# RMS norms of a one-core kernel: token sums as four columns, root and inverse on 128x4, spread with the repeated inverse as stationary operand

## The chip, the cores and the metric

The kernel runs on 1 core of one Trainium2 chip, as a single launch. The metric is the device time of that core in microseconds. The median of 3 runs before the change is 3313.32 us (3313.13 to 3313.98). TensorE (PE) multiplies; VectorE (DVE), ScalarE (ACT) and GpSimd (POOL) do the elementwise work; SyncE (SP) issues the weight transfers.

## The reference, cut to what matters

Three transformer blocks over 512 tokens of width 1024, in float32. What the change touches is the norm, which stands ahead of or behind nearly every branch:

```python
def rms_norm(x, g):
    xf = x.astype(jnp.float32)
    y = xf * lax.rsqrt(jnp.mean(xf * xf, axis=-1, keepdims=True) + EPS)
    return (y * g.astype(jnp.float32)).astype(x.dtype)

# one half of a layer of the second part
h = h + 0.5 * rms_norm_2(swiglu(rms_norm_2(h, g[4]), ffn_w13[i, 1], ffn_w2[i, 1]), g[5])
gate = jax.nn.sigmoid(rms_norm_2(h, g[6]) @ ple_w_gate[i])
h = h + rms_norm_2(gate * (p[i] @ ple_w_proj[i]), g[7])
```

Between these stand dilated, stick-breaking and memory attention, a gated convolution MLP, a gMLP mixer and an RWKV-7 mixer; the change leaves them as they are.

## The kernel before, in words

Activations lie features by tokens: eight tiles of 128 features x 512 tokens. Every weight product is three products of a high and a low part (`xh`, `xl` with `wh`, `wl`), so PE runs a long row of 128x512 matmuls (line 510, helper `linear`; lines 1219 to 1221, helper `Woven`). Weights come in 1 MB chunks into two slots of `raw`; ACT makes `wh` (line 315), DVE makes `wl` (line 331).

The order is written out by hand: each stage appends to a block of every engine, and semaphores with constants join them. Each engine works its own row of instructions strictly in order.

A norm is an object `Pass`. Its mean is over features, so over partitions and over the eight tiles. Where the producer of the tiles already added up squares (`by="before"`), seven tiles' squares stand in one 128x512 tile (`rs` or `sums_p`) and the last tile's squares in another (`tmp`). A second kind (`by="tensor"`) squares all eight tiles itself, and PE adds up each.

Eleven passes have the form that the change touches (`self.quarters`); they stand at about 559, 928, 1295, 1586, 1954, 2015, 2384, 2400, 2866, 3235 and 3295 us of the span:

- `sum_quarters` (lines 804 to 809, matmul at 807): four matmuls with 32 columns of ones as stationary operand and 128 tokens of squares as moving operand. Token block b gives partitions 32b to 32b+31 of a 128x128 result in bank 7, each sum 32 times over. All matmuls here are float32, and the trace shows two loads and two matmuls for each one issued.
- `square_root` (line 770, ACT) on 128x128, out of PSUM; `invert` (line 862, DVE), a reciprocal on 128x128.
- `spread` (lines 830 to 839, matmul at 837): four matmuls of 32 rows of ones with 32 rows of inverses give the inverse on all partitions, 128x512, in banks 2 and 3; a wait stands between the first two and the last two.
- `keep_busy` (line 980, matmul at 983): dummy 128x256 matmuls that fill PE while it waits for the inverse: three ahead of `spread`, and some more behind it.

Then DVE multiplies tile by tile with the spread inverse (lines 882, 885, 912), ACT takes the high part (778, 1028, 2407), DVE the low part (934, 1077), and PE starts on the first tile. In some passes POOL adds to the residual (919).

Other norms (`deferred`) already have the column form that the change brings: `add_up` (matmul at line 800), mean, root and inverse on 128x4 (866, 774, 868), diagonal and one product with ones (870, 841). They are not touched, but show operations of the same shape.

Two of the eleven passes stand in `Beside` (line 2387), where PE fills its wait not with dummies but with the products of the embedding projection, eight units of six matmuls. One (`to_hn`, line 2646, second pass) is `by="tensor"`: for each of eight tiles ACT squares (line 765), PE adds up (807), and from the third tile on PE runs two dummy matmuls ahead of each sum.

Of the kernel before, what the change touches and what calls it, by code (L numbers as in the profile page):

```python
# [219 lines left out]
def _build(nc, io, ctx, block):  # L220
# [388 lines left out]
    class Stage:  # L609
# [3 lines left out]
        def act(self, act):  # L613
            pass
# [95 lines left out]

    REPEAT = P // TB
    last_squares = [(None, act_steps)]

    class Pass:
# [3 lines left out]
        def __init__(self, number, source, gain, split=None, plain=None, onto=False, tokens=EVERY, by="tensor",  # L718
                     deferred=False, total=None, stat=0):
            self.source, self.gain, self.split, self.plain, self.onto, self.tokens = source, gain, split, plain, onto, tokens  # L720
            self.total = rs if total is None else total
            self.n_tok, self.by = tokens.stop - tokens.start, by
            self.blocks = slice(tokens.start // P, tokens.stop // P)
            self.quarters = by in ("before", "tensor") and not deferred and tokens == EVERY
            self.sums = ps[:, 7, 0:P] if self.quarters else ps[:, 7 - 5 * number, self.blocks]
            self.last, squares_by = last_squares[0]
            self.squares_sem, self.squared = squares_by.sem, squares_by.total
            self.scale = (ps[:, 2:4, P:3 * P] if self.quarters else
                          ps[:, 6 - 3 * number, tokens])
# [5 lines left out]
            for s, n in ((n_square, 0 if by == "before" else KD), (n_add, KD - 1 if by == "vector" else 0),  # L735
                         (n_sum, KD if by == "tensor" else 1), (n_mean, 0 if self.quarters else 1), (n_root, 1),
                         (n_scale, 1 if self.quarters else 2), (n_spread, 4 if self.quarters else 1),
                         (n_value, 0 if deferred else KD), (n_onto, KD if onto else 0), (n_high, KD if split else 0),
                         (n_low, KD if split else 0)):
                self.at[s] = s.total  # L740
                s.total += n
# [5 lines left out]
        def view(self, x):  # L747
            return x.rearrange("p (a t) -> p a t", a=2) if self.quarters else x

# [29 lines left out]

        def act(self, act, before):  # L780
            act.wait_ge(chunks_used, self.multiplied)
            act.wait_ge(psum_read.sem, self.evicted)
            act.wait_ge(dve_steps.sem, self.summed)
            for t in range(0 if self.by == "before" else KD):
                self.square(act, t, before)
            self.square_root(act)
            if self.split:
                for t in range(KD):
                    self.high(act, t)

        def sum_tile(self, pe, t):
            self.wait(pe, n_square, t + 1)
            if self.quarters:
                self.sum_quarters(pe, self.scratch(t % 2), t == 0, t == KD - 1).then_inc(n_sum.sem, 1)
                return
            self.add_up(pe, self.scratch(t % 2), t == 0, t == KD - 1)
# [6 lines left out]

        def sum_quarters(self, pe, squares, first_one, last_one):
            for b in range(TB):
                rows = slice(REPEAT * b, REPEAT * b + REPEAT)
                last = nc.tensor.matmul(ps[rows, 7, 0:P], table("ones")[:, 0:REPEAT], squares[:, b * P:(b + 1) * P],
                                        start=first_one, stop=last_one, skip_group_check=True)
            return last

        def sum_up(self, pe, between=0):
            if self.quarters and self.by == "before":
                pe.wait_ge(dve_steps.sem, self.summed - 1)
                self.sum_quarters(pe, self.total, True, False)
                pe.wait_ge(self.squares_sem, self.squared)
                self.sum_quarters(pe, self.last, False, True).then_inc(n_sum.sem, 1)
                return
# [24 lines left out]

        def pe(self, pe, idle, between):
            if not self.quarters:
                pe.wait_ge(psum_read.sem, self.evicted)
            self.sum_up(pe, between)
            if self.quarters:
                pe.wait_ge(psum_read.sem, self.evicted)
# [10 lines left out]
        def invert(self, dve):  # L859
            if self.quarters:  # L860
# [13 lines left out]
        def value(self, dve, t):  # L874
            g = vec[:, self.gain + t:self.gain + t + 1]
            if t == 0:
                self.wait(dve, n_spread, 4 if self.quarters else 1)
            if (self.onto or self.split) and t >= 2:
# [28 lines left out]
        def gained(self, dve, t):  # L907
            if t == 0:
                self.wait(dve, n_spread, 4 if self.quarters else 1)
            if t >= 2:  # L910
# [74 lines left out]
    class Deferred(Stage):  # L985
# [45 lines left out]
        def pe(self, pe):  # L1031
            if self.post:
# [97 lines left out]
    def split_norm(gain, source=None, split=x_split, tokens=EVERY):  # L1130
        return Norms(dict(source=h if source is None else source, gain=gain, split=split, tokens=tokens), idle=(3, 4), lead=5)

# [245 lines left out]
    def _(dve):  # L1378
        nc.vector.memset(spare[:, 0:2], 1.0)
        nc.vector.memset(spare[:, 3:4], REPEAT * REPEAT * EPS)  # L1380
        nc.vector.memset(spare[:, 2:3], GN_EPS).then_inc(halved, 1)
# [1005 lines left out]
    class Beside(Deferred):  # L2387
# [8 lines left out]

        def act(self, act):
            act.wait_ge(chunks_used, self.multiplied)
            act.wait_ge(psum_read.sem, self.evicted)
            act.wait_ge(dve_steps.sem, self.two.summed)  # L2400
            self.post.square_root(act)
            self.lots.high(act, 0)
# [9 lines left out]
        def pe(self, pe):  # L2412
# [209 lines left out]
    def rwkv():  # L2622
# [22 lines left out]

        to_hn = Norms(post(ybuf, 1, 1), dict(source=h, gain=gain(1, 2), plain=hn), idle=(3, 7, 6), between=2)
        hn_pass = to_hn.passes[1]
# [1078 lines left out]
    def _(pe):  # L3726
# [3 lines left out]
        pe.wait_ge(psum_read.sem, last.evicted)  # L3730
        keep_busy(pe, 3)
        last.spread(pe)
# [90 lines left out]
```

## Time and profile before

| what | value |
|---|---|
| median of 3 runs | 3313.32 us |
| span of the profiled execution (first to last instruction) | 3311.6 us |
| granted TensorE clock, mean | 0.995 |
| PE busy | 3236.2 us (98%) |
| DVE busy | 1780.1 us (54%) |
| ACT busy | 1214.9 us (37%) |
| POOL busy | 97.2 us (3%) |
| matmuls of line 510, share of the chain that ended last | 70% |

The profile gives the profiled execution no total of its own beside the span; the median of the runs lies 1.7 us above the span, which is what start and end outside the first and last instruction take. PE's share counts the dummy matmuls too, and the busy time of pipelined matmuls overlaps, so 98% does not say that PE never waits. The granted clock is 1.0 for 2.4 GHz and 0.50 for 1.2 GHz.

### The profile page before, as it was taken

Reading aid. Unit: us, or ns where it says so; the run is one execution under the profiler, and the core shown is the slowest. Engines: PE = TensorE matmul, PEld = TensorE weight load, DVE = VectorE, ACT = ScalarE, POOL = GpSimd, SP = SyncE. Lnnn points to the kernel's source line nnn. Section 1 sums busy time; section 2 is a strip of 40 time slices with the busy share of each in tenths; the row PEclk is TensorE's granted clock in tenths of the full one; section 3 lists DMA queues with packets and bytes.
Section 4 is the critical chain, followed back from the end, with each engine's and each line's share of the span. In section 5 each row is a group of like instructions: output and inputs, shape, how many; then the busy total and the mean of one; then the engine's idle time right before and its main releaser. Section 6 shows DMA issues by size and latency. Waiting matters only on the chain.

```text
span 3311.6 us, 46921 instructions
## 1 busy us (share of the span) xinstructions
PE 3236.2 (98%) x20532; PEld 2650.2 (80%) x20532; DVE 1780.1 (54%) x2113; ACT 1214.9 (37%) x1532; POOL 97.2 (3%) x100
## 2 busy tenths in 40 slices
PE   8999999999999999999999999999999999999998
PEld 6878786888878888988788887888777787788886
DVE  5446665776254434464644357443476665754437
ACT  3347643322242223342422234222235564332224
POOL 2000000000000001000100011000000000100001
PEclk9999999999999999999999999999999999999999
DMA  5211131222322223222222222222212100122231
GB/s 189 84 52 64 64 140 42 99 102 87 104 90 102 85 96 112 102 77 102 83 102 93 88 99 89 95 97 88 92 70 73 50 4 16 70 103 101 87 104 64
DMA packets 45980, 286.49 MB, mean 87 GB/s; under 512 B 5952, under 2 KB 6224, under 8 KB 19920
## 3 DMA queue, kind: packets, MB, share of 16 engines
q1 hardware_dynamic: 44240, 280.34, 24.2%
q0 software_dynamic: 1536, 3.15, 0.4%
q8 instruction: 162, 2.65, 0.3%
q14 instruction: 42, 0.34, 0.0%
HBM read 278.22 MB, written 2.10 MB: 85 GB/s over the span
## 4 chain that ended last, share of the span: by engine, by line
PE 80%; DVE 5%; ACT 1%; issue 1%; DVEq 0%; ACTq 0%
PE ps L510 70%; PE ps L3245 3%; PE ps L3283 1%; PE ps L1219 1%; DVE wl L331 1%; PE ps L983 1%; DVE xl L2719 1%; PE ps L1220 0%; PE ps L1221 0%; ACT wh L315 0%; PE ps L2549 0%; DVE xl L1077 0%; PE ps L837 0%; DVE tmp L2727 0%; PE ps L3290 0%
## 5 line engine op out<-in xcount | busy, mean ns | idle before, releaser
L510 PE MATMUL ps<-xh,wh 128*128 128x512 f32 (+1 forms) x2464 | 966.6, 393 | 23.3 <-DVE xl L1077 10.6
L510 PE MATMUL ps<-xl,wh 128*128 128x512 f32 (+1 forms) x2464 | 947.1, 391 | 0.3
L510 PE MATMUL ps<-xh,wl 128*128 128x512 f32 (+1 forms) x2464 | 921.3, 391 | 0.0
L331 DVE TENSOR_TENSOR wl<-raw,wh 128x2048 fp32r<-128x2048 f32 (+1 forms) x284 | 591.4, 2082 | 452.8 <-ACT wh L315 452.6
L315 ACT CAST wh<-raw 128x2048 fp32r<-128x2048 f32 (+2 forms) x281 | 487.7, 1735 | 299.0 <-PE ps L510 292.8
L510 PEld LDWEIGHTS ps<-xh,wh 128*128 128x128 f32 (+1 forms) x2464 | 463.1, 188 | 132.6 <-issue 28.0
L510 PEld LDWEIGHTS ps<-xl,wh 128*128 128x128 f32 (+1 forms) x2464 | 462.6, 188 | 101.5 <-DVE xl L1077 2.9
L510 PEld LDWEIGHTS ps<-xh,wl 128*128 128x128 f32 (+1 forms) x2464 | 462.6, 188 | 99.1 <-issue 1.0
L510 PE MATMUL ps<-hid_h,wh 128*128 128x512 f32 x880 | 342.8, 390 | 0.0
L510 PE MATMUL ps<-hid_l,wh 128*128 128x512 f32 x880 | 342.4, 389 | 0.0
L510 PE MATMUL ps<-hid_h,wl 128*128 128x512 f32 x880 | 342.4, 389 | 0.0
L2202 ACT ACTIVATE tmp<-tmp 128x512 f32<-128x512 f32 x88 | 55.7, 633 | 539.5 <-DVE tmp L2210 539.4
L2210 DVE TENSOR_TENSOR tmp<-ps,rs 128x512 f32<-128x512 f32 x88 | 60.8, 691 | 292.4 <-PE ps L510 287.0
L510 PEld LDWEIGHTS ps<-hid_h,wh 128*128 128x128 f32 x880 | 165.2, 188 | 35.3 <-DVE wl L331 1.4
L510 PEld LDWEIGHTS ps<-hid_l,wh 128*128 128x128 f32 x880 | 165.2, 188 | 34.4
L510 PEld LDWEIGHTS ps<-hid_h,wl 128*128 128x128 f32 x880 | 165.2, 188 | 34.3
L919 POOL TENSOR_TENSOR h<-tmp,h 128x512 f32<-128x512 f32 x42 | 66.5, 1613 | 2743.1 <-DVE tmp L912 2743.1
L1270 DVE COPY ybuf<-ps 128x512 f32<-128x512 f32 x40 | 27.7, 692 | 178.0 <-PE ps L510 156.4
L2195 DVE TENSOR_TENSOR hid_l<-tmp,hid_h 128x512 fp32r<-128x512 f32 x110 | 76.2, 693 | 75.5 <-ACT hid_h L2191 75.5
L1314 ACT ACTIVATE tmp<-ybuf 128x512 f32<-128x512 f32 x35 | 22.1, 632 | 246.4 <-DVE ybuf L1270 192.1
L2191 ACT CAST hid_h<-tmp 128x512 fp32r<-128x512 f32 x110 | 68.3, 621 | 86.6 <-DVE tmp L2215 67.1
L510 PE MATMUL ps<-wh,xh 128*128 128x256 f32 x352 | 94.7, 284 | 0.1
(437 smaller groups left out, 3996.2 us busy)
## 6 DMA issues: line engine op xcount, KB each, us to landing
raw<-in_up SPq DMA_DIRECT2D x88, 1024.0 KB, 4.7
raw<-in_down SPq DMA_DIRECT2D x64, 704.0 KB, 4.0
raw<-in_up_c SPq DMA_DIRECT2D x22, 1024.0 KB, 4.7
raw<-in_down_c SPq DMA_DIRECT2D x16, 704.0 KB, 4.1
raw<-in_gates SPq DMA_DIRECT2D x8, 1024.0 KB, 4.7
raw<-in_gv SPq DMA_DIRECT2D x8, 1024.0 KB, 4.8
raw<-in_gu SPq DMA_DIRECT2D x8, 1024.0 KB, 4.8
raw<-in_gout SPq DMA_DIRECT2D x8, 1024.0 KB, 4.7
```

The lines of the kernel that those rows point to most:

```text
L315: nc.scalar.copy(wh[:, slot, 0:w], raw[:, slot, 0:w]).then_inc(hi_ready, 1)
L331: nc.vector.tensor_tensor(wl[:, slot, 0:w], raw[:, slot, 0:w], wh[:, slot, 0:w].bitcast(F32), ALU.subtract).then_inc(lo_ready, 1)
L510: last = nc.tensor.matmul(out, stationary, moving, start=(fresh and q == 0), stop=(t == kt - 1 and half == per - 1 and q == 2), skip_group ...
L919: nc.gpsimd.tensor_tensor(dst, self.scratch(2 + t % 2), dst, ALU.add).then_inc(n_onto.sem, 1)
L983: nc.tensor.matmul(ps[:, bank_, 0:2 * P], table("ident"), const[:, 0:2 * P], start=True, stop=True)
L1219: nc.tensor.matmul(ps[:, b, :], wh[0:r, slot, wc], hi[0:r], start=(t == 0), stop=False, skip_group_check=True)
L2191: nc.scalar.copy(hid_h[:, k, tokens], tmp[:, 2 + u, tokens]).then_inc(act_steps.sem, 1)
L2195: nc.vector.tensor_tensor(hid_l[:, k, tokens], tmp[:, 2 + u, tokens], hid_h[:, k, tokens].bitcast(F32), ALU.subtract).then_inc(dve_steps.s ...
L2202: nc.scalar.activation(tmp[:, u, :], tmp[:, u, :], ACT.Silu).then_inc(act_steps.sem, 1)
L2210: nc.vector.tensor_tensor(tmp[:, u, :], products[0], rs[:, :], ALU.mult).then_inc(dve_steps.sem, 1)
L2719: nc.vector.tensor_tensor(xl[:, t, :], tmp[:, t % 4, :], xh[:, t, :].bitcast(F32), ALU.subtract).then_inc(x_used.sem, 1)
L3245: last = nc.tensor.matmul(out(e, c), left(lhs, e, c), right(rhs, e, c), start=(n == 0), stop=(n == len(pairs) - 1), skip_group_check=True)
```

## The change

Each of the eleven passes keeps its place. The sums become four columns: the squares of 128 tokens are the stationary operand and one column of ones the moving one, so the result is 128 tokens x 4. Root and reciprocal work on 128x4. The spread takes one column of the inverse, repeated 128 times by a stride of zero, as stationary operand and the identity as moving one, four times, with no wait between them. The dummies ahead of the spread go from three to one. In ACT's row the root is put ahead of the waits for the last chunk and the last eviction. In `Beside` one unit of products instead of two stands ahead of the spread, and the other moves behind it. Line numbers shift a little: the sum is line 808 there, the root 769, the spread 835, the dummies 981, the embedding products 1217 to 1219.

```diff
...
-            self.quarters = by in ("before", "tensor") and not deferred and tokens == EVERY
-            self.sums = ps[:, 7, 0:P] if self.quarters else ps[:, 7 - 5 * number, self.blocks]
+            self.by_columns = by in ("before", "tensor") and not deferred and tokens == EVERY
+            self.sums = ps[:, 7, 0:TB] if self.by_columns else ps[:, 7 - 5 * number, self.blocks]
...
         def square_root(self, act):
-            if self.quarters:
+            if self.by_columns:
                 self.wait(act, n_sum, KD if self.by == "tensor" else 1)
-                nc.scalar.activation(self.total[:, 0:P], self.sums, ACT.Sqrt, scale=REPEAT * REPEAT / D,
+                nc.scalar.activation(self.root, self.sums, ACT.Sqrt, scale=1.0 / D,
                                      bias=spare[:, 3:4]).then_inc(n_root.sem, 1)
...
         def act(self, act, before):
+            if self.by == "before":
+                self.square_root(act)
             act.wait_ge(chunks_used, self.multiplied)
             act.wait_ge(psum_read.sem, self.evicted)
             act.wait_ge(dve_steps.sem, self.summed)
...
-        def sum_quarters(self, pe, squares, first_one, last_one):
+        def sum_columns(self, pe, squares, first_one, last_one):
             for b in range(TB):
-                rows = slice(REPEAT * b, REPEAT * b + REPEAT)
-                last = nc.tensor.matmul(ps[rows, 7, 0:P], table("ones")[:, 0:REPEAT], squares[:, b * P:(b + 1) * P],
-                                        start=first_one, stop=last_one, skip_group_check=True)
+                last = nc.tensor.matmul(self.sums[:, b:b + 1], squares[:, b * P:(b + 1) * P], table("ones")[:, 0:1],
+                                        start=(first_one and b == 0), stop=last_one, skip_group_check=True)
             return last
...
         def spread(self, pe):
-            if self.quarters:
+            if self.by_columns:
                 self.wait(pe, n_scale, 1)
-                for n, b in enumerate((0, 2, 1, 3)):
-                    if n == 2:
-                        self.wait(pe, n_spread, 2)
-                    rows = slice(REPEAT * b, REPEAT * b + REPEAT)
-                    nc.tensor.matmul(ps[:, 2 + b // 2, P + b % 2 * P:2 * P + b % 2 * P], table("ones")[rows, :],
-                                     self.total[rows, P:2 * P], start=True, stop=True, skip_group_check=True).then_inc(n_spread.sem, 1)
+                for b in range(TB):
+                    nc.tensor.matmul(ps[:, 2 + b // 2, P + b % 2 * P:2 * P + b % 2 * P], self.inverse[:, b:b + 1].broadcast_to([P, P]),
+                                     table("ident"), start=True, stop=True, skip_group_check=True).then_inc(n_spread.sem, 1)
...
         def invert(self, dve):
-            if self.quarters:
+            if self.by_columns:
                 self.wait(dve, n_root, 1)
-                nc.vector.reciprocal(self.total[:, P:2 * P], self.total[:, 0:P]).then_inc(n_scale.sem, 1)
+                nc.vector.reciprocal(self.inverse, self.root).then_inc(n_scale.sem, 1)
...
         def split_act(self, act):
             if self.here:
                 self.here(act)
+            if self.post:
+                self.post.square_root(act)
             act.wait_ge(chunks_used, self.multiplied)
             act.wait_ge(psum_read.sem, self.evicted)
             act.wait_ge(dve_steps.sem, self.two.summed)
-            if self.post:
-                self.post.square_root(act)
...
                 pe.wait_ge(psum_read.sem, self.evicted)
-                keep_busy(pe, 3)
+                keep_busy(pe, 1)
                 self.post.spread(pe)
...
             self.lots.products(pe, 1, 0, 2)
-            self.lots.products(pe, 2, 0, 2)
             self.post.spread(pe)
-            for unit in range(3, KD):
+            for unit in range(2, KD):
                 self.lots.products(pe, unit, 0, 2)
...
```

PE's row in the two passes of `to_hn` before the change (`rs` and `tmp` are squares, `const` the ones or the dummies' operands):

```order
L807 MATMUL ps<-rs_56,const_58 32x128 x4
L807 MATMUL ps<-tmp_57,const_58 32x128 x4
L983 MATMUL ps<-const_58 128x256 x3
L837 MATMUL ps<-rs_56,const_58 128x128 x4
L983 MATMUL ps<-const_58 128x256 x6
L807 MATMUL ps<-tmp_57,const_58 32x128 x8
L983 MATMUL ps<-const_58 128x256 x2
L807 MATMUL ps<-tmp_57,const_58 32x128 x4
```

And the same place in the changed kernel:

```order
L808 MATMUL ps<-const_58,rs_56 128x1 x4
L808 MATMUL ps<-const_58,tmp_57 128x1 x4
L981 MATMUL ps<-const_58 128x256
L835 MATMUL ps<-const_58,stats_59 128x128 x4
L981 MATMUL ps<-const_58 128x256 x6
L808 MATMUL ps<-const_58,tmp_57 128x1 x8
L981 MATMUL ps<-const_58 128x256 x2
L808 MATMUL ps<-const_58,tmp_57 128x1 x4
```

Nothing moved here but the count of dummies ahead of the spread, three to one; the two dummies ahead of each later sum stay.

PE's row around the spread in the first `Beside` before the change (`pt_h`, `pt_l` are the embedding's halves). The two sums stand three rows further up, ahead of unit 1:

```order
L1219 MATMUL ps<-pt_h_7512,wh_51 128x512
L1220 MATMUL ps<-pt_l_7513,wh_51 128x512
L1221 MATMUL ps<-pt_h_7512,wl_52 128x512
L1219 MATMUL ps<-pt_h_7512,wh_51 128x512
L1220 MATMUL ps<-pt_l_7513,wh_51 128x512
L1221 MATMUL ps<-pt_h_7512,wl_52 128x512
L1219 MATMUL ps<-pt_h_7512,wh_51 128x512
L1220 MATMUL ps<-pt_l_7513,wh_51 128x512
L1221 MATMUL ps<-pt_h_7512,wl_52 128x512
L837 MATMUL ps<-rs_56,const_58 128x128 x4
```

And in the changed kernel, from the sums to the spread:

```order
L808 MATMUL ps<-const_58,rs_56 128x1 x4
L808 MATMUL ps<-const_58,tmp_57 128x1 x4
L1217 MATMUL ps<-pt_h_7509,wh_51 128x512
L1218 MATMUL ps<-pt_l_7510,wh_51 128x512
L1219 MATMUL ps<-pt_h_7509,wl_52 128x512
L1217 MATMUL ps<-pt_h_7509,wh_51 128x512
L1218 MATMUL ps<-pt_l_7510,wh_51 128x512
L1219 MATMUL ps<-pt_h_7509,wl_52 128x512
L835 MATMUL ps<-const_58,stats_59 128x128 x4
```

The spread stands six matmuls behind the sums instead of twelve; those six stand behind it now, and PE's work in the stage stays the same but for the forms of sum and spread.

## Rows read from the trace of the kernel before

**Rows 1.** The page: chain that ended last, by engine

```profile
PE 80%; DVE 5%; ACT 1%; issue 1%; DVEq 0%; ACTq 0%
```

**Rows 2.** Line 862, the reciprocals: duration ns min/median/max, first and last start

```profile
L862 DVE RECIPROCAL rs<-rs x9: 952/953/954, 560.5 to 3236.2; 128x128 f32<-128x128 f32 x9
L862 DVE RECIPROCAL sums_p<-sums_p x2: 954/954/954, 2015.9 to 3296.0; 128x128 f32<-128x128 f32 x2
```

**Rows 3.** Timeline, pass at 559: start us, us, engine, line [idle before <-releaser]

```profile
558.83 0.42 PE L807 MATMUL ps<-rs,const 128*32 128x128 f32 x8
...
559.42 0.43 PE L807 MATMUL ps<-tmp,const 128*32 128x128 f32 x8 [0.16 <-ACT tmp L1326]
...
559.99 0.37 ACT L770 ACTIVATE rs<-ps,spare 128x128 f32<-128x128 f32 x1 [0.63 <-PE ps L807]
560.50 0.95 DVE L862 RECIPROCAL rs<-rs 128x128 f32<-128x128 f32 x1 [1.85 <-ACT rs L770]
...
561.50 1.07 PE L837 MATMUL ps<-rs,const 32*128 32x128 f32 x8 [0.17 <-DVE rs L862]
...
562.65 1.41 DVE L885 SCALAR_TENSOR_TENSOR tmp<-h,vec,ps 128x512 f32<-128x512 f32 x2 [1.20 <-PE ps L837]
```

**Rows 4.** Lines 774 and 868, root and reciprocal of the untouched norms

```profile
L774 ACT ACTIVATE stats<-stats x10: 203/205/206, 31.6 to 3266.4; 128x4 f32<-128x4 f32 x9, 128x2 f32<-128x2 f32 x1
L868 DVE RECIPROCAL stats<-stats x10: 166/178/179, 31.8 to 3266.6; 128x4 f32<-128x4 f32 x9, 128x2 f32<-128x2 f32 x1
```

**Rows 5.** Timeline, column sums of an untouched norm among weight products, 3265 to 3266

```profile
3264.95 0.39 PE L510 MATMUL ps<-xh,wl 128*128 128x512 f32 x1
3265.17 0.94 PE L800 MATMUL ps<-const,rs 128*128 128x1 f32 x8
...
3265.98 2.57 PE L510 MATMUL ps<-xh,wl 128*128 128x512 f32 x10
3266.16 0.16 DVE L866 TENSOR_SCALAR stats<-ps 128x4 f32<-128x4 f32 x1 [1.23 <-PE ps L800]
```

**Rows 6.** Timeline of PE, four 128x128 by 128x128 products at 2591

```profile
2591.47 1.09 PE L3283 MATMUL ps<-const,x_area 128*128 128x128 f32 x8 [0.24 <-DVE x_area L3018]
```

**Rows 7.** Timeline, pass at 1295, whose last tile is copied out of PSUM

```profile
1294.49 0.42 PE L807 MATMUL ps<-tmp,const 128*32 128x128 f32 x8 [0.39 <-ACT tmp L1326]
...
1295.24 0.37 ACT L770 ACTIVATE rs<-ps,spare 128x128 f32<-128x128 f32 x1 [0.81 <-DVE ybuf L1270]
```

**Rows 8.** Timeline, second pass of to_hn

```profile
2392.19 0.43 PE L807 MATMUL ps<-tmp,const 128*32 128x128 f32 x8
2392.54 0.73 PEld L983 LDWEIGHTS ps<-const 128*128 128x128 f32 x4 [0.20 <-issue]
...
2399.27 0.42 PE L807 MATMUL ps<-tmp,const 128*32 128x128 f32 x8
...
2399.76 0.37 ACT L770 ACTIVATE rs<-ps,spare 128x128 f32<-128x128 f32 x1 [1.47 <-PE ps L807]
```

**Rows 9.** Timeline, the first Beside

```profile
1953.83 0.39 PE L1221 MATMUL ps<-pt_h,wl 128*128 128x512 f32 x1
...
1954.73 0.50 PE L1219 MATMUL ps<-pt_h,wh 128*128 128x512 f32 x1
...
1957.39 0.39 PE L1221 MATMUL ps<-pt_h,wl 128*128 128x512 f32 x1
...
1958.72 0.50 PE L1219 MATMUL ps<-pt_h,wh 128*128 128x512 f32 x1
...
1974.80 0.75 DVE L1077 SCALAR_TENSOR_TENSOR xl<-h,vec,xh 128x512 fp32r<-128x512 f32 x1 [0.31 <-ACT xh L2407]
...
1976.12 0.62 PE L510 MATMUL ps<-xl,wh 128*128 128x512 f32 x2
```

**Rows 10.** Stretches: us, busy us of PE, PEld, DVE, ACT, POOL, PEclk, DMA share

```profile
2405.50:2408.80 3.30, 1.18 (x5) 1.04 (x6) 3.23 (x7) 0.75 (x2) 0.00 (x0) 1.00 0.01 2
2409.00:2415.50 6.50, 5.57 (x14) 4.07 (x13) 6.36 (x12) 1.27 (x3) 0.00 (x0) 0.50 0.01 3
```

More of the change, by code:

```diff
@@ L723, in __init__ @@
             self.blocks = slice(tokens.start // P, tokens.stop // P)
-            self.quarters = by in ("before", "tensor") and not deferred and tokens == EVERY
-            self.sums = ps[:, 7, 0:P] if self.quarters else ps[:, 7 - 5 * number, self.blocks]
+            self.by_columns = by in ("before", "tensor") and not deferred and tokens == EVERY
+            self.sums = ps[:, 7, 0:TB] if self.by_columns else ps[:, 7 - 5 * number, self.blocks]
             self.last, squares_by = last_squares[0]
             self.squares_sem, self.squared = squares_by.sem, squares_by.total
-            self.scale = (ps[:, 2:4, P:3 * P] if self.quarters else
+            self.scale = (ps[:, 2:4, P:3 * P] if self.by_columns else
                           ps[:, 6 - 3 * number, tokens])
@@ L735, in __init__ @@
             for s, n in ((n_square, 0 if by == "before" else KD), (n_add, KD - 1 if by == "vector" else 0),
-                         (n_sum, KD if by == "tensor" else 1), (n_mean, 0 if self.quarters else 1), (n_root, 1),
-                         (n_scale, 1 if self.quarters else 2), (n_spread, 4 if self.quarters else 1),
+                         (n_sum, KD if by == "tensor" else 1), (n_mean, 0 if self.by_columns else 1), (n_root, 1),
+                         (n_scale, 1 if self.by_columns else 2), (n_spread, 4 if self.by_columns else 1),
                          (n_value, 0 if deferred else KD), (n_onto, KD if onto else 0), (n_high, KD if split else 0),
@@ L747, in view @@
         def view(self, x):
-            return x.rearrange("p (a t) -> p a t", a=2) if self.quarters else x
+            return x.rearrange("p (a t) -> p a t", a=2) if self.by_columns else x
         def wait_result(self, engine, t):
@@ L783, in act @@
             act.wait_ge(dve_steps.sem, self.summed)
-            for t in range(0 if self.by == "before" else KD):
-                self.square(act, t, before)
-            self.square_root(act)
+            if self.by != "before":
+                for t in range(KD):
+                    self.square(act, t, before)
+                self.square_root(act)
             if self.split:
@@ L792, in sum_tile @@
             self.wait(pe, n_square, t + 1)
[L793 to L794 removed]
+            if self.by_columns:
+                self.sum_columns(pe, self.scratch(t % 2), t == 0, t == KD - 1).then_inc(n_sum.sem, 1)
                 return
@@ L802, in add_up @@
             last.then_inc(n_sum.sem, 1)
-        def sum_quarters(self, pe, squares, first_one, last_one):
+        def sum_columns(self, pe, squares, first_one, last_one):
             for b in range(TB):
-                rows = slice(REPEAT * b, REPEAT * b + REPEAT)
-                last = nc.tensor.matmul(ps[rows, 7, 0:P], table("ones")[:, 0:REPEAT], squares[:, b * P:(b + 1) * P],
-                                        start=first_one, stop=last_one, skip_group_check=True)
+                last = nc.tensor.matmul(self.sums[:, b:b + 1], squares[:, b * P:(b + 1) * P], table("ones")[:, 0:1],
+                                        start=(first_one and b == 0), stop=last_one, skip_group_check=True)
             return last
         def sum_up(self, pe, between=0):
-            if self.quarters and self.by == "before":
+            if self.by_columns and self.by == "before":
                 pe.wait_ge(dve_steps.sem, self.summed - 1)
-                self.sum_quarters(pe, self.total, True, False)
+                self.sum_columns(pe, self.total, True, False)
                 pe.wait_ge(self.squares_sem, self.squared)
-                self.sum_quarters(pe, self.last, False, True).then_inc(n_sum.sem, 1)
+                self.sum_columns(pe, self.last, False, True).then_inc(n_sum.sem, 1)
                 return
@@ L843, in pe @@
         def pe(self, pe, idle, between):
-            if not self.quarters:
+            if not self.by_columns:
                 pe.wait_ge(psum_read.sem, self.evicted)
             self.sum_up(pe, between)
-            if self.quarters:
+            if self.by_columns:
                 pe.wait_ge(psum_read.sem, self.evicted)
@@ L876, in value @@
             if t == 0:
-                self.wait(dve, n_spread, 4 if self.quarters else 1)
+                self.wait(dve, n_spread, 4 if self.by_columns else 1)
             if (self.onto or self.split) and t >= 2:
@@ L908, in gained @@
             if t == 0:
-                self.wait(dve, n_spread, 4 if self.quarters else 1)
+                self.wait(dve, n_spread, 4 if self.by_columns else 1)
             if t >= 2:
@@ L1130, in split_norm @@
     def split_norm(gain, source=None, split=x_split, tokens=EVERY):
-        return Norms(dict(source=h if source is None else source, gain=gain, split=split, tokens=tokens), idle=(3, 4), lead=5)
+        return Norms(dict(source=h if source is None else source, gain=gain, split=split, tokens=tokens), idle=(1, 4), lead=5)
     s_high, s_low = roles("split_highs", "split_lows")
@@ L1379, in _ @@
         nc.vector.memset(spare[:, 0:2], 1.0)
-        nc.vector.memset(spare[:, 3:4], REPEAT * REPEAT * EPS)
+        nc.vector.memset(spare[:, 3:4], EPS)
         nc.vector.memset(spare[:, 2:3], GN_EPS).then_inc(halved, 1)
@@ L2397, in act @@
         def act(self, act):
+            self.post.square_root(act)
             act.wait_ge(chunks_used, self.multiplied)
@@ L2644, in _ @@
                 nc.gpsimd.memset(x[64:P, 0:2, :].bitcast(F32), 0.0).then_inc(lora_rows_clear, 1)
-        to_hn = Norms(post(ybuf, 1, 1), dict(source=h, gain=gain(1, 2), plain=hn), idle=(3, 7, 6), between=2)
+        to_hn = Norms(post(ybuf, 1, 1), dict(source=h, gain=gain(1, 2), plain=hn), idle=(1, 7, 6), between=2)
         hn_pass = to_hn.passes[1]
@@ L3730, in _ @@
         pe.wait_ge(psum_read.sem, last.evicted)
-        keep_busy(pe, 3)
+        keep_busy(pe, 1)
         last.spread(pe)
```

4 lines of the change are left out of this document (1 added, 3 removed).

## Prediction

> **What bounds the kernel now.** I read the page's chain first: 80% of what ended last is PE and 5% DVE [rows 1], so the time is PE's row of weight products plus the places where PE waits. Then the single lines of the norm, for how many passes there are: nine reciprocals on `rs` and two on `sums_p`, 0.95 us each, eleven passes [rows 2]. Then the timeline of one pass, to see whether the norm is hidden. It is not: from the last square on, every step names the one before it as its releaser. The sum starts at 559.42, the root at 559.99, the reciprocal at 560.50, the spread at 561.50, the first tile's scaling at 562.65 [rows 3]. That is 3.23 us in a line, and PE does only dummies meanwhile. What follows (scaling, high part, low part, first product) hangs on 562.65, and PE is the bound again behind it, so what such a pass gains or loses moves all that follows. This holds for nine passes. In the two of `Beside` PE has real products to do all along [rows 9], and there only PE's own work counts.
>
> **Root and reciprocal.** The root took 0.37 us on 128x128 [rows 3]; on 128x4 in the untouched norms it takes 0.205 [rows 4]: -0.165. Those read SBUF and the new one reads PSUM, so the price lies between 0.205 and 0.37; I take 0.205, since the form is otherwise the same. The reciprocal goes from 0.953 to 0.178 [rows 2, 4]: -0.775. Its form is exact. Together -0.94 a pass.
>
> **The sums on the path.** The old groups are short: eight matmuls in 0.43 us, and the root starts 0.57 us behind their start [rows 3]. The new form already stands in an untouched norm [rows 5]: eight passes of 128x128 by one column hold PE from 3265.17 to 3265.98, 0.81 us, and their reader on DVE starts 0.99 us behind their start. The reader is now ACT, which started 0.14 us after the end of the old sum, where DVE in rows 5 started 0.05 after it (3265.17 + 0.94 = 3266.11): 0.09 more. And the squares are now the stationary operand, whose load can't begin before they are there: some 0.04. So 1.12 us in place of 0.57: +0.55, bounded by 0.99 (nothing more) and about 1.2 (the 1.09 us of eight 128x128 passes [rows 6] and ACT's 0.14).
>
> The Trainium skill (TensorE: Matmul & The Clock Gate, "Part 3: Packing small matmuls — row/col tiling") speaks against this part: products that use 32 columns of the array each run side by side, and one that takes all 128 columns has no such neighbour. Its section on LDWEIGHTS has the load cost go with the columns of the stationary operand, 107 ns for 128 and so 27 for 32. By that the added time on PE would be 8 x 0.08 = 0.64 us a sum, an estimate from that page; rows 3 and 5 make it 0.4 to 0.55, since the old sum does not shrink as far as the page lets it.
>
> **The first group of sums.** It holds seven tiles and was out of the way early. At 559 it starts at 558.83 and the second at 559.42 [rows 3]; with 0.81 us it ends at 559.64, so the second waits 0.22 more. In the other passes the two groups stand about 0.8 us or more apart and nothing is added (0.8 us in rows 7 too, as I read that timeline).
>
> **The spread.** Before, from its start to its reader: 561.50 to 562.65, 1.15 us, with the wait in its middle [rows 3]. The new one is four full products of 128 columns, for which rows 6 have 1.09 us, and 0.08 to the reader as before: 1.17, +0.02. No row shows a stationary operand with stride zero. From below, nothing can be gained beyond some 0.1 (the loads alone). From above, I bound a pass by the slowest regular one near here, the dummies of 256 columns: four in 0.86 us, 0.214 each [rows 8] (0.73 us for four loads, of which the last begins 0.64 behind the first). Eight of them would be 1.71 instead of 0.86, +0.85 a spread. I take the value of rows 6, the nearest form.
>
> **Dummies three to one.** One dummy is 0.43 us. Between the end of the sum and the spread now lie 0.14 + 0.205 + 0.14 + 0.178 + 0.05 = 0.71 us (the steps between engines from rows 3), so a single one ends before the spread is due and three would not. It costs nothing, and it saves a delay that three would bring.
>
> **ACT's root ahead of its waits.** In passes whose last tile is copied out of PSUM the root waited for that copy: 1294.49 to 1295.24, 0.75 us instead of 0.57 [rows 7]. There the new sum comes 0.37 later (1.12 - 0.75), not 0.55, since the wait for the copy is gone or covered. Four passes are of this kind (1295, 1586, 2384, 2866). What is behind the root in ACT's row is the 1.9 us cast of weights, which is done well ahead of the first high part; it moves by 0.2 to 0.4 us and stays hidden.
>
> **The pass that adds on PE (2387 to 2400).** Sums follow one another at (2399.27 - 2392.19)/5 = 1.416 us, of which 0.86 are dummies and 0.35 the sum, the rest a gap in PE's row [rows 8]. With 0.81 for the sum and no gap (rows 5 show none on either side) it is 1.67. The sums of rows 8 have no idle time in front of them, so PE already is the slower one and not the squares, and it is clearly so with longer sums: six periods, 6 x 0.254 = +1.52. Then the last sum: the root came 0.49 us behind its start [rows 8], now 1.12: +0.63. Less 0.94 and plus 0.02 for the spread: +1.23.
>
> **Beside.** PE's products follow at 0.23 us. The two sums held PE from 1953.83 + 0.23 to 1954.73, 0.67 us [rows 9]; now 1.62: +0.95. The spread held it from 1957.62 to 1958.72, 1.10 us; now about 0.9: -0.2. The chain through the inverse doesn't matter: the root can start at 1956.0, the inverse is there at about 1956.6, and PE reaches the spread, behind the sums and one unit (1.36 us), at about 1957.05. Behind it the chain through the weights' cast on ACT and their low part on DVE shifts the scaling by up to 1 us, and PE by +0.75; the last low part was there at 1975.55, PE took it at 1976.12 [rows 9], so 0.57 of slack covers the difference. Result: +0.75 each, +1.5 for two. Moving the unit behind the spread brings nothing, since PE does the same work.
>
> **The sum.** Passes 928, 2015, 3295: -0.94 + 0.55 + 0.02 = -0.37, three times -1.1. Pass 559: -0.37 + 0.22 = -0.15. Four copy passes: -0.94 + 0.37 + 0.02 = -0.55, together -2.2. Pass 2400: +1.23. Two Beside: +1.5. Total -0.7 us: the profiled execution's span of 3311.6 goes to 3310.9, and with the 1.7 us that the median lies above the span, 3312.6 us. The gain in root and reciprocal, 9 x 0.94 = 8.5 us, is given back by sums that are longer on the path (4.3), by the adding pass's longer periods (1.5) and by Beside (1.5), and 0.2 each by the first group and the spreads.
>
> **Rivals.**
> *The one-column sums cost the path nothing.* If loads of the squares ran as short as the old packed ones, each of nine passes would keep -0.9 and the adding pass and Beside would lose nothing: -8.3, so 3305.0. For it: the sum is only four results. Against it: rows 5, 0.94 us for the very form.
> *The clock falls in a norm.* From 2405.5 on PE had little to do (1.18 us busy of 3.30), and from 2409.0 to 2415.5 the granted clock stood at 0.50, the lower level of 1.2 GHz [rows 10]. The changed passes put 1.6 us of one-column sums and about 0.3 us of idle time where there were three dummies. If that is too little work to hold 2.4 GHz, PE-bound products behind a norm run at half pace for a time as long as in rows 10, 6.5 us, and lose half of it, 3.3 us. It decides the sign from the first such fall on (-0.7 + 3.3); I price it at four of the eight passes that PE-bound work follows: +13 - 0.7, so 3325.6. Against it: no pass of before but 2400's has the lower level behind it, and PE does not stand idle longer than it did. No row says whether one-column matmuls hold the clock. The Trainium skill (the same page, "Part 4: PE-mode transpose") says of transposes that they don't count as busy in the same way; it has nothing on one-column products. The phase also matters: the low stretch of rows 10 comes at another moment after the change, and may shrink or grow by up to 2 us with no meaning.
> *Repeated column or root from PSUM slow.* Spreads at +0.85 in nine passes and roots at 0.37 in nine: +7.7 + 1.5 - 0.7 = +8.5, so 3321.8. For it: no row shows either. Against it: the operand's address pattern is plain, and 128x128 loads differ little over the trace.
>
> **How the numbers follow.** Forecast 0.80, the sums free 0.05, the clock 0.09, the slow spread 0.06. A measurement tells 0.2% from no change, 6.6 us. The forecast's own terms leave +-0.1 us in nine sums, up to 1.5 in the roots, 1 in the adding pass and 2 for the clock's phase: 3309.0 to 3316.5. A little toward either side makes the range 3308.5 to 3317.5. Faster by over 0.2% (under 3306.7) takes the sums' rival and little else: 0.05. Slower (over 3319.9) takes the most of the other two and single mishaps: 0.11. Same: 0.84.
>
> **What the new profile would show.** Reciprocals of 0.18 us and roots of 0.2 us on 128x4. From a second sum's start to the root about 1.1 us, and from there to the first scaling about 1.7. Sums in the adding pass at 1.67 us. Beside longer by 0.7 to 0.8 us from the first sum to the first gate product. The clock at 1.00 in all passes but the one place. I am wrong if the root starts within 0.8 us of the sum's start, if a spread takes more than 1.4 us, if the adding pass keeps 1.4 us, or if 0.50 appears behind a norm.

## The result, and the profile after

| kernel | median us | runs | ratio to before, 95% interval |
|---|---|---|---|
| before | 3312.68 (3310.52 to 3313.98) | 10 | |
| changed | 3322.54 (3313.70 to 3330.98) | 10 | 1.0028 (1.0019 to 1.0036) |

The change makes the kernel 9.9 us slower, where 0.7 us faster (3312.6 us) was forecast, and it scatters the runs over 17 us where they lay within 3.5. The profiled execution took 3321.13 us (span 3319.3), with a mean granted clock of TensorE of 0.992 against 0.995. The run list gives each run's clock: the three runs at 3313.70 to 3314.11 have 0.996, the seven from 3320.95 up have 0.989 to 0.992. That points at the clock.

An ordinary pass gains, as it was meant to. This is the pass at 926 in the timeline of the changed kernel (start us, us, engine, line); [rows 3] is its like:

```profile
925.50 1.05 PE L808 MATMUL ps<-const,tmp 128*128 128x1 f32 x8 [0.72 <-ACT tmp L1324]
...
926.59 0.26 ACT L769 ACTIVATE stats<-ps,spare 128x4 f32<-128x4 f32 x1 [1.14 <-PE ps L808]
926.98 0.18 DVE L860 RECIPROCAL stats<-stats 128x4 f32<-128x4 f32 x1 [2.26 <-ACT stats L769]
927.22 1.16 PE L835 MATMUL ps<-const,stats 128*128 128x128 f32 x8
...
928.41 2.06 DVE L883 SCALAR_TENSOR_TENSOR h<-h,vec,ps 128x512 f32<-128x512 f32 x3 [1.25 <-PE ps L835]
```

From the second sum's start to the first scaling it is 2.91 us. The same pass took 3.23 us before (927.47 to 930.70), as the one in [rows 3] did. The root comes 1.09 us behind the sum (1.12 forecast), takes 0.26 (0.205 forecast, 0.37 the other bound), the reciprocal 0.18, spread to reader 1.19 us.

The loss is in the adding pass. PE and ACT in its middle in the changed kernel, which [rows 8] answer:

```profile
2394.62 1.71 PE L808 MATMUL ps<-const,tmp 128*128 128x1 f32 x8
...
2396.18 2.05 PE L981 MATMUL ps<-const 128*128 128x256 f32 x4
2396.42 0.63 ACT L764 ACTIVATE tmp<-h 128x512 f32<-128x512 f32 x1 [2.78 <-PE ps L808]
...
2398.03 1.71 PE L808 MATMUL ps<-const,tmp 128*128 128x1 f32 x8
...
2408.27 1.71 PE L808 MATMUL ps<-const,tmp 128*128 128x1 f32 x8
...
2410.31 0.18 DVE L860 RECIPROCAL stats<-stats 128x4 f32<-128x4 f32 x1 [12.71 <-ACT stats L769]
```

A tile takes 2398.03 - 2394.62 = 3.41 us, where it took 1.416, and DVE sits idle for 12.71 us ahead of the second reciprocal. From the first reciprocal of `to_hn` (2383.06, in the same timeline) to the second it is 27.25 us; before it was 2384.57 to 2400.16, 15.59 us. Those 11.7 us are more than the whole loss. Some of them come back right behind the pass, where the low stretch of [rows 10] is gone: from the first product of line 510 to the first copy out of PSUM on DVE it is 35.61 us (2418.09 to 2453.70), and it was 37.51 (2407.62 to 2445.13). The stretches of the changed kernel (columns as in [rows 10]; PEclk is the granted clock) say why the pass is long:

```profile
2390.00:2413.00 23.00, 23.00 (x84) 20.61 (x83) 7.90 (x11) 3.41 (x6) 0.00 (x0) 0.50 0.13 46
2413.50:2440.00 26.50, 23.48 (x101) 18.09 (x100) 22.89 (x42) 6.85 (x9) 0.00 (x0) 1.00 0.00 1
```

From 2390 on PE counts as busy in every microsecond of the pass, and its granted clock is 0.50, the level of 1.2 GHz, to the end of it. PE does not look idle in any busy share; only the clock column and the durations show it (a sum's eight matmuls take 1.71 us; at the full level they took 0.95 to 1.05). Nor had PE done less ahead of the fall than before the change. These are the stretches from the last spread to it, first in the changed kernel, then the like in the kernel before:

```profile
2384.30:2389.50 5.20, 4.76 (x31) 4.01 (x29) 4.91 (x8) 1.94 (x4) 0.00 (x0) 1.00 0.00 0
2386.60:2392.20 5.60, 4.69 (x36) 3.18 (x34) 5.38 (x9) 1.89 (x3) 0.00 (x0) 1.00 0.01 3
```

PE was busy for 4.76 of 5.20 us where it had been busy for 4.69 of 5.60, with the same six dummies in it; what differs is the form of the sums. Then the clock fell in the one and stayed at 1.00 in the other.

`Beside` behaves as worked out. PE in the changed kernel:

```profile
1951.70 0.95 PE L808 MATMUL ps<-const,rs 128*128 128x1 f32 x8
...
1954.89 1.05 PE L835 MATMUL ps<-const,stats 128*128 128x128 f32 x8
...
1963.99 0.39 PE L510 MATMUL ps<-xh,wh 128*128 128x512 f32 x1
```

From the sums' turn to the first gate product it is 12.29 us; before it was 11.59 (from 1954.06, 0.23 behind the last product of [rows 9] ahead of the sums, to the first product of line 510 at 1965.65): +0.70, with +0.75 forecast.

### The profile page after: what moved, and what is told of

Same layout as the page of the kernel before. It is cut to its first block, busy times and chain, and to the rows that moved or that the text cites. A ratio compares the mean times of both kernels' runs of the same rounds, so it can differ in the third digit from the quotient of the medians.

```text
span 3319.3 us, 46841 instructions
## 1 busy us (share of the span) xinstructions
PE 3249.7 (98%) x20496; PEld 2676.7 (81%) x20496; DVE 1771.4 (53%) x2113; ACT 1214.0 (37%) x1532; POOL 97.3 (3%) x100
## 4 chain that ended last, share of the span: by engine, by line
PE 81%; DVE 4%; ACT 1%; issue 1%; DVEq 0%; ACTq 0%
PE ps L510 70%; PE ps L3242 3%; PE ps L3280 1%; PE ps L808 1%; PE ps L981 1%; DVE wl L331 1%; PE ps L1217 1%; DVE xl L2716 1%; PE ps L1219 0%; PE ps L1218 0%; ACT wh L315 0%; PE ps L2546 0%; PE ps L835 0%; DVE xl L1075 0%; DVE tmp L2724 0%
```

## The experiments

In all of them the new form and the old one stand side by side, chosen by the number of the pass in order of time (0 to 10; 7 is the adding pass, 4 and 9 are the two of `Beside`). Where a pass is in the old form its three dummies ahead of the spread are too; the root keeps its new place in ACT's row in all of them, which makes 3.37 us instead of 3.40 from sum to scaling in the old pass at 1295 (adding pass only, 1294.81 to 1298.18). Theory: the one-column sums don't hold TensorE's clock, and in the adding pass, where they alternate with dummies, it stays down. Rival: PE simply has more to do.

| kernel | median us | range | ratio to before, 95% interval |
|---|---|---|---|
| adding pass old | 3313.92 | 3311.19 to 3316.39 | 1.0004 (0.9995 to 1.0013) |
| adding pass only | 3323.35 | 3321.72 to 3327.65 | 1.0036 (1.0023 to 1.0049) |
| changed, ones 128 wide | 3313.84 | 3312.95 to 3318.21 | 1.0009 (1.0000 to 1.0018) |
| changed, three dummies | 3326.58 | 3320.11 to 3328.40 | 1.0038 (1.0025 to 1.0050) |
| path passes wide | 3309.22 | 3306.83 to 3311.03 | 0.9991 (0.9982 to 0.9999) |
| path passes, one column | 3313.07 | 3308.28 to 3315.94 | 1.0003 (0.9994 to 1.0012) |
| adding pass only, 128 wide | 3314.01 | 3311.31 to 3316.93 | 1.0006 (0.9997 to 1.0014) |
| Beside only | 3312.68 | 3310.68 to 3314.57 | 1.0004 (0.9995 to 1.0013) |
| adding pass only, 32 wide | 3314.27 | 3310.94 to 3314.93 | 1.0003 (0.9994 to 1.0012) |
| adding pass only, 64 wide | 3313.91 | 3311.45 to 3316.80 | 1.0005 (0.9996 to 1.0014) |
| adding pass only, four dummies | 3320.96 | 3317.78 to 3324.32 | 1.0025 (1.0016 to 1.0034) |
| path passes wide, three dummies | 3312.21 | 3310.62 to 3313.30 | 0.9998 (0.9989 to 1.0007) |

The kernel before, run beside them, had medians of 3312.42 (first four), 3312.41 (next four) and 3312.18 us (last four). Differences below are between medians; those of one or two us lie close to what the intervals allow.

**The adding pass put back**

```diff
-    CHOICE = lambda k: True
+    CHOICE = lambda k: k != 7
```

> The changed kernel with one of its eleven passes put back: the adding pass (second of to_hn) sums with four packed 32-column groups and has root, inverse, spread and dummies as before. Theory 'clock': one-column sums don't hold the granted clock, and in the adding pass, where sums and dummies take half of PE's time each, it stays at 0.50 for the whole pass; put back, the pass has its 1.42 us a tile, no 0.50 inside it, and the median is 3311 to 3314 us with runs within 4 us of each other. Rival 'PE time alone': the loss is longer sums on PE everywhere; then only some 1.3 us come back: 3320 to 3322 us.

3313.92 us: 8.6 us of the 9.9 come back. The runs span 5.2 us, not the 4 expected. A stretch of its profile over the pass reads 1.00:

```profile
2387.00:2403.00 16.00, 14.84 (x117) 9.40 (x116) 14.18 (x19) 5.73 (x10) 0.00 (x0) 1.00 0.10 31
```

**The adding pass alone**

```diff
-    CHOICE = lambda k: True
+    CHOICE = lambda k: k == 7
```

with `Beside` in the old order.

> The kernel before with only the adding pass (second of to_hn) in the new form; the other ten passes and the order in Beside as before. Clock theory: it shows nearly the whole loss and the scatter, some runs near 3314 and others at 3322 or more, median 3318 to 3325 us, and in a slow one 3.4 us a tile at a granted clock of 0.50. Rival, PE time alone: 1.7 us a tile at 1.00, 3313.5 to 3315 us, no scatter.

One pass of eleven makes the whole loss, 10.9 us, and its profile has the same 0.50:

```profile
2392.00:2414.00 22.00, 22.00 (x80) 19.74 (x79) 7.94 (x11) 3.54 (x7) 0.00 (x0) 0.50 0.14 48
```

The expected scatter didn't come: all five runs were long.

**Ones 128 columns wide, in all passes**

```diff
-                last = nc.tensor.matmul(self.sums[:, b:b + 1], squares[:, b * P:(b + 1) * P], table("ones")[:, 0:1],
+                last = nc.tensor.matmul(ps[:, 7, 128 * b:128 * (b + 1)], squares[:, b * P:(b + 1) * P], table("ones")[:, 0:128],
```

> The changed kernel with the moving operand of every sum 128 columns of ones instead of 1, each sum 128 times over; the root reads every 128th column. The loads are the same, and eight passes took 0.81 us with one column and about 0.9 by the 128x128 products, so PE's time hardly grows (1.75 us a tile in the adding pass). Clock theory: streaming columns hold the clock; no 0.50 in the adding pass, median 3312 to 3315 us, runs within 4 us. Rival, PE time alone, or loads being what matters: 3321 to 3324 us as the changed kernel.

This tells the theories apart best: the same loads, the same number of matmuls, more columns streamed, so no less work on PE, and 8.7 us less than the changed kernel. (The runs span 5.3 us, again more than the 4 expected.) A stretch over the adding pass and two of its sums:

```profile
2390.00:2403.00 13.00, 12.72 (x88) 11.51 (x87) 9.79 (x13) 4.68 (x8) 0.00 (x0) 1.00 0.16 55
```

```profile
2396.08 1.05 PE L833 MATMUL ps<-const,tmp 128*128 128x128 f32 x8
...
2397.84 1.05 PE L833 MATMUL ps<-const,tmp 128*128 128x128 f32 x8
```

1.76 us a tile at a clock of 1.00, with PE busy for 12.72 of 13.00 us. One thing changes beside the width: the four sums lie 128 columns apart in PSUM instead of side by side, and no run separates the two. The granted clock is read from the trace, though, so that it is the clock and not PSUM that stretches the pass is shown; the layout could only be a rival for why it falls.

**Three dummies again**

```diff
-    WAITING = 1
+    WAITING = 3
```

> The changed kernel with three dummies ahead of the spread again in nine passes (Beside has none). Clock theory: the adding pass still falls, so most of the loss stays: 3319 to 3325 us, and each of the other passes starts its spread some 0.5 us later. If the missing dummies alone were the cause, the clock would stay and the time be 3313 to 3316 us.

3326.58 us, above the expected range: the missing dummies are not the cause. Whether bringing them back costs 4 us more, as the medians say, is not shown: five runs lie between 3320.11 and 3328.40, inside the spread of the changed kernel's ten.

**The eight path passes, 128 wide and one column**

```diff
-    CHOICE = lambda k: True
+    CHOICE = lambda k: k not in (4, 7, 9)
```

> Eight of eleven passes in the new form with 128-column ones; the adding pass and both Beside passes (sums, spread and order of the units) as before the change. If the new form gains where the norm is on the path (0.4 to 0.5 us a pass, as the traces show) and loses only where PE's own time counts, and wide ones hold the clock: about 3.5 us faster than before, 3308 to 3311 us. If the eight passes gain nothing: 3312 to 3314 us.

> The same eight passes with one-column ones. Clock theory: in some runs the granted clock falls behind one or two of these passes (1 to 3 us each), so the median lies 0 to 2 us above that of the 128-column kernel and the runs scatter more: 3309 to 3313 us. Rival, the clock matters in the adding pass alone: no difference, both 3308 to 3311 us.

Wide: 3309.22 us, 13 less than the changed kernel and 3.2 less than before, though against before the interval (0.9982 to 0.9999) only just leaves out 1. One column: 3313.07. The 3.9 us between them are more than was expected. The one-column kernel's profile shows a clock below 1.00 at three places that hold such a pass; the wide one's stands at 1.00 there. First the one-column kernel, with the stretch behind the adding pass as its last line:

```profile
540.00:575.00 35.00, 34.87 (x160) 29.01 (x158) 24.38 (x34) 13.53 (x19) 0.00 (x0) 0.95 0.18 61
1275.00:1300.00 25.00, 24.88 (x118) 21.00 (x117) 9.39 (x10) 7.18 (x7) 1.23 (x1) 0.93 0.48 168
2000.00:2025.00 25.00, 24.77 (x112) 20.19 (x112) 18.78 (x26) 11.73 (x17) 4.61 (x4) 0.93 0.14 50
2405.00:2425.00 20.00, 18.02 (x67) 14.34 (x68) 18.02 (x33) 4.35 (x7) 0.00 (x0) 0.83 0.01 2
```

and the wide one:

```profile
540.00:575.00 35.00, 34.11 (x162) 27.87 (x162) 24.42 (x35) 13.52 (x19) 0.00 (x0) 1.00 0.16 61
1275.00:1300.00 25.00, 24.52 (x122) 20.34 (x121) 8.81 (x10) 7.19 (x7) 0.65 (x1) 1.00 0.46 158
2000.00:2025.00 25.00, 24.33 (x117) 19.28 (x116) 19.48 (x27) 12.54 (x18) 4.72 (x4) 1.00 0.17 62
2405.00:2425.00 20.00, 17.95 (x75) 13.72 (x76) 18.08 (x33) 4.34 (x7) 0.00 (x0) 1.00 0.00 2
```

The last lines are a warning against reading the 3.9 and the 3.2 us as the price and the gain of the passes themselves. The adding pass is in the old form in both kernels, yet behind it the one-column kernel has the low stretch of [rows 10] and the wide one has none. From the first product there to the first copy out of PSUM the kernel before takes 37.51 us, the one-column kernel 37.62 (2405.88 to 2443.50) and the wide one 35.59 (2405.94 to 2441.53), so some 2 us of either difference come from there in these profiles. It is not one profile's luck: seven of the wide kernel's eleven runs have a mean clock of 0.997, which none of the 33 runs of the kernel before beside it has (0.994 to 0.996). Why the fall stays out behind an unchanged pass was not tested. The time of arrival alone does not decide it, since both kernels reach the place at the same time. The wide passes' own gain, from the second sum to the first scaling, is 0.38 us in each of the four whose last tile is copied (3.02 against 3.40) and 0.20 in the one at 928; at 559, 2015 and 3295, where the second sum waits behind the first, it is 0.00, 0.10 and 0.02 from the first sum's start. Together that is about 1.8 us.

What one fall costs on the path shows in the changed kernel, whose spread at 1294 fell into one:

```profile
1292.20 1.05 PE L808 MATMUL ps<-const,tmp 128*128 128x1 f32 x8
...
1293.92 2.07 PE L835 MATMUL ps<-const,stats 128*128 128x128 f32 x8
...
1296.03 0.75 DVE L910 SCALAR_TENSOR_TENSOR tmp<-ybuf,vec,ps 128x512 f32<-128x512 f32 x1 [2.17 <-PE ps L835]
```

3.83 us from sum to scaling. The wide kernel takes 3.02 there, shown in the last experiment.

**The adding pass alone, 128 wide**

```diff
-    CHOICE = lambda k: True
+    CHOICE = lambda k: k == 7
```

with the wide ones.

> The kernel before with only the adding pass in the new form, with 128-column ones. It isolates PE's longer sums from the clock: 1.75 us a tile instead of 1.42, six tiles +2.0, the last sum +0.6, root and reciprocal -0.9: about 1.7 us slower than before, 3313.5 to 3315.5 us, where the same pass with one column took 3323.35. If its loss were PE's time, it would be 3322 or more.

3314.01 us, +1.6: PE's longer sums without the fall in the pass. Against the one-column form of the same pass it is 9.3 us less, so of that pass's 10.9 us some 1.6 are PE's time and 9.3 the clock's. The profile gives the same order: from the first reciprocal of `to_hn` to the first product behind the adding pass it is 25.18 us (2384.96 to 2410.14), 2.1 more than the 23.05 before, and 35.60 us (2384.38 to 2419.98) with one column.

**Beside alone**

```diff
-    CHOICE = lambda k: True
+    CHOICE = lambda k: k in (4, 9)
```

> The kernel before with only the two Beside passes in the new form (one-column sums, spread with the repeated inverse), the order of the units as before: two units ahead of the spread. PE does 0.95 us more for the two sums and 0.2 less for the spread, each time: +0.7 us a pass from the first sum to the first gate product, 3313.5 to 3315 us. If Beside is bound by the chain through the inverse instead, it gets shorter: 3311 to 3312 us.

3312.68 us, +0.3: less than expected, and inside what the runs can tell (0.9995 to 1.0013). Its timeline does show the term: sums' turn at 1953.82, and 12.3 us to the first gate product against 11.59. So the term is seen in the trace, but the medians don't confirm it. The 12.3 us are those of the changed kernel too, so moving a unit behind the spread did nothing, as forecast.

**Narrower ones: 32 and 64 columns, in the adding pass alone**

```diff
-table("ones")[:, 0:128]
+table("ones")[:, 0:32]
```

> The kernel before with only the adding pass in the new form, ones 32 columns wide. PE's loads are the same as with 1 or 128 columns. If what holds the clock is streamed columns, 32 are a quarter of 128 and the pass, half of whose time is dummies, may still fall: 3317 to 3325 us with 3.4 us a tile in a slow profile. If any width over one suffices: 3313 to 3316 us, 1.7 us a tile.

> The same with 64 columns of ones. Streamed columns hold the clock: nearer to the 128-column kernel than to the one-column one, 3313 to 3317 us. If only full 128 do: 3320 to 3325 us.

3314.27 and 3313.91 us: both like 128, whose median was 3314.01. I had thought 32 might not do. Sums in the 32-column kernel:

```profile
2394.74 0.97 PE L833 MATMUL ps<-const,tmp 128*128 128x32 f32 x8
...
2396.49 0.97 PE L833 MATMUL ps<-const,tmp 128*128 128x32 f32 x8
```

**Four dummies between one-column sums**

```diff
-idle=(1, 7, 6), between=2)
+idle=(1, 7, 6), between=4)
```

> The kernel before with only the adding pass in the new form with one-column ones, and four dummies ahead of each of its sums instead of two. More streamed columns between the sums (two thirds of the time) should hold the clock: 2.6 us a tile at 1.00, six times 1.15 more than before and 0.3 less at the end, 3318 to 3320.5 us with little scatter. If one-column sums bring the clock down whatever stands between them: 5 us a tile and 3330 us or more.

3320.96 us, just above the expected range. The stretch over the pass, and two sums:

```profile
2391.00:2410.00 19.00, 18.75 (x108) 16.98 (x108) 9.41 (x12) 4.24 (x8) 0.00 (x0) 0.91 0.15 55
```

```profile
2398.51 0.95 PE L833 MATMUL ps<-const,tmp 128*128 128x1 f32 x8
...
2401.13 0.95 PE L833 MATMUL ps<-const,tmp 128*128 128x1 f32 x8
```

The clock fell once (0.91 over the stretch) and came back: 2.62 us a tile with sums of 0.95, the full level. With two dummies it did not come back before the pass's end. By the medians four dummies are quicker than two, by 2.4 us; the two intervals overlap, but the profiles agree: 25.21 us from reciprocal to reciprocal (2385.06 to 2410.27) against 27.82 (2384.38 to 2412.20). The wide ones are quicker than either.

**Three dummies, path passes wide**

```diff
-    WAITING = 1
+    WAITING = 3
```

> The eight path passes in the new form with 128-column ones, the adding pass and Beside old, and three dummies ahead of each spread instead of one. Three dummies take 1.3 us where the inverse is there after 0.8: each spread starts some 0.5 us later, 8 times, so 3312.5 to 3314 us against 3309.22 with one. If the dummies cost nothing: 3308 to 3310.5 us.

3312.21 us, just below the expected range and 3.0 more than with one. The same pass in both, one dummy first:

```profile
1294.11 1.16 PE L833 MATMUL ps<-const,tmp 128*128 128x128 f32 x8
...
1295.93 1.16 PE L869 MATMUL ps<-const,stats 128*128 128x128 f32 x8 [0.23 <-DVE stats L898]
...
1297.13 0.75 DVE L948 SCALAR_TENSOR_TENSOR tmp<-ybuf,vec,ps 128x512 f32<-128x512 f32 x1 [1.25 <-PE ps L869]
```

and three:

```profile
1295.54 1.16 PE L833 MATMUL ps<-const,tmp 128*128 128x128 f32 x8
...
1297.83 1.05 PE L869 MATMUL ps<-const,stats 128*128 128x128 f32 x8
...
1298.93 0.75 DVE L948 SCALAR_TENSOR_TENSOR tmp<-ybuf,vec,ps 128x512 f32<-128x512 f32 x1 [1.62 <-PE ps L869]
```

With one, PE waits for DVE at the spread; with three the spread has no such wait and comes later: from sum to scaling it is 3.39 us instead of 3.02, and 8 x 0.37 = 3.0, as much as the medians differ. That match is partly luck, since the profile with three dummies also has a clock below 1.00 behind the adding pass, which the one with one dummy has not.

## Why the prediction was wrong, point by point

- *The pass that adds on PE* is the step that failed. It had +1.23 us, worked out from durations at the full clock. With one column the pass costs +10.9 (the pass alone). PE's longer sums are +1.6 of that (128 wide), and 9.3 is the clock at 0.50 through the pass: 3.41 us a tile where 1.67 was forecast. I had priced 0.81 us of sum and 0.86 of dummies as if the dummies between one-column sums would hold the clock.
- *The rival on the clock* named the mechanism and gave it 0.09. It stood in the wrong place: behind the passes, 3.3 us a fall, weighed as four falls. In the adding pass PE's own work sets the pace, so there the fall lasted as long as the pass. That its time of 3325.6 us lies near the measured 3322.54 is luck: it was added up from four falls that did not happen so. The argument against it, that PE does not stand idle longer than before, was true and did not matter: PE was busy for 4.76 of 5.20 us ahead of the fall and for 23.00 of 23.00 us at the lower level. Its smaller form exists too, in three of the eight path passes with one-column sums, and the changed kernel's spread at 1293.92 took 2.07 us for 1.16.
- *Root and reciprocal* held, the reciprocal at 0.18 us, the root at 0.26, 0.06 more than taken. The forecast said that its form was otherwise that of the untouched root. It is not: the new root reads PSUM and also takes `spare` as a bias, as its row shows, and the untouched one does neither, so which of the two costs the 0.06 us is open.
- *The sums on the path* held: 1.09 us for 1.12. *The spread*: 1.19 for 1.17, so the stationary operand of stride zero cost nothing that shows.
- *The first group of sums* was forecast to add nothing beyond the pass at 559. In the one-column kernel the second sum at 2015 starts 0.91 us behind the first (2012.16 to 2013.07), where it was 0.79 (2014.07 to 2014.86), so a little was added there too.
- *Dummies three to one* held, and the delay saved, 0.37 us, is as large as the gain of a whole pass (0.32 us at 928, 0.38 with wide ones at 1295).
- *Beside* held in the traces: +0.70 for +0.75.
- *The eight path passes* had a sum of -3.45 us in the forecast. The median with wide ones, -3.2, looks like it, but by luck: the passes' own rows give -1.8, and some 2 us come from the clock behind the old adding pass.
- *The rivals on free sums and a slow spread* are out: rows above.

Without the fall in the adding pass, then, the forecast was near: all passes new with wide ones came to 3313.84, +1.4 to before, with -0.7 forecast. The parts say where most of the missing 2 us lie: the eight path passes gave -1.8 for -3.45, the adding pass +1.6 for +1.23, the two `Beside` +1.4 for +1.5 by the timelines. The wide sums' extra 0.1 us ahead of every root is part of the first. The clock outside the passes is not in these parts, and it differs where nothing was changed: from 35 to 50 us, ahead of every pass of the new form, it reads 0.89 in the profile before and 1.00 in the changed kernel's. Open too is what decides whether a run of the changed kernel falls: three of ten did not, by their clock, while the adding pass alone was long in five of five, and none of the kernels was built to tell that apart.

## What to carry to other kernels

An operation that keeps PE busy need not keep its clock: look at the clock column over each stretch where a form changes, above all where PE alone sets the pace, since a low clock there stretches the very loop in which it fell. If a small matmul's loads set its time, widen its moving operand: here 32 or 128 columns instead of one cost 0.02 to 0.1 us a sum and saved about 9 us. When the wait that dummies fill becomes shorter, count them again: they stand in PE's row ahead of the work that waits. And before a gain of a few us is put down to the lines that were changed, compare the clock where nothing changed.

## What the runs showed that I had not expected

- With 32 columns of ones the clock stayed up in the adding pass as with 128 (3314.27 and 3314.01 us); with one column it did not (3323.35), with the same loads and the same 128x128 stationary operands.
- At the lower level the loads slow as well: eight took 2.04 us in the adding pass and 0.97 at the full one, in this row of the changed kernel's timeline and its like at 2388.54:

```profile
2394.19 2.04 PEld L808 LDWEIGHTS ps<-const,tmp 128*128 128x128 f32 x8
```

- The root on 128x4 takes 0.263 us out of PSUM with a bias operand and 0.205 out of SBUF without one [rows 4].
